# Prelude of a decoder layer: how the squares of the input are summed, what is loaded first, and how the first two projection tiles advance

## The chip, the cores and the metric

The kernel runs on one core of a Trainium2 chip, as one launch. The metric is the time on the device in microseconds (us), from start to end of the launch; smaller is better. Every input is float32, and the inputs lie in the chip's memory (HBM) when the launch starts.

## The reference

One hybrid decoder layer over 1024 tokens of width 1024. The conditioning vector `c` gives six modulation vectors. Then come an RMS norm with modulation, one input projection to 2240 columns, two kinds of attention (8 stick-breaking heads and 4 latent-attention heads), an output projection, a second norm with modulation, and a SwiGLU feed-forward of width 2816. Only its first lines touch this change:

```python
mod = jax.nn.silu(c) @ w_ada[l] + b_ada[l]
shift1, scale1, gate1, shift2, scale2, gate2 = [m[:, None, :] for m in jnp.split(mod, N_MOD, axis=-1)]
h = rms_norm(x, norm_attn[l]) * (1.0 + scale1) + shift1
proj = h @ w_in[l]
```

## The kernel before

The activations are kept transposed: `x_in[:, j, :]` is chunk j of eight, 128 channels on the partitions by 1024 tokens. A product of two float32 operands at close to full precision is made of three faster ones: an operand is split into a high part (a copy rounded to `fp32r`) and a low part (the difference), and the kernel sums high·high, high·low and low·high. `WH`/`WL` are the parts of a weight tile of 128 output channels, each with two buffers; `hH`/`hL` are those of the normalized input. A projection tile is 8 chunks x 3 products x 2 halves of 512 tokens = 48 matmuls, into two of the eight PSUM banks of `ps`.

Each engine runs its own list of instructions in the written order, and semaphores tie the lists together. What the prelude does before the first projection tile, in that order:

- SyncE (SP) starts the loads: three small ones, `x_in` in four parts of 1 MB, the raw weights of tiles 0 and 1 (`raw`, 0.5 MB each), then `ada1`, the four parts (2 MB each) of the modulation weights for `shift1` and `scale1`. Part g serves chunks 2g and 2g+1.
- ScalarE (ACT) squares each chunk as it comes (line 658). VectorE (DVE) adds the squares up in `sqs` (line 1112), seven additions. TensorE (PE) turns the sum by eight transposes (line 1721) and DVE reduces it (line 1122) to the mean square `ms` of each token (line 1124).
- GpSimd (POOL) takes the power -1/2 (line 557), DVE lays it on diagonals (line 1129), and PE spreads it over all partitions by two matmuls with ones (line 1749). DVE multiplies each chunk by it (`normalize`, line 1142).
- For part g, PE multiplies `silu(c)` with the modulation weights (`mod1_rows`, line 1734), DVE copies the result (`mod1_copy`, line 1119), PE sums the copy into columns by matmuls whose stationary side is a 128x128 block and whose moving side is one column of ones (`mod1_columns`, line 1741), and DVE makes shift and scale of it (`scale_shift`, lines 1136 and 1139). `mod1_rows(g)` waits for `scale_shift(g-2)`.
- Before `mod1_rows(0)` PE runs `WARM` = 40 small bf16 matmuls on the identity (line 1745), whose result nobody reads. A like group of 44 stands at line 1897, much later.
- For each chunk j, ACT writes `hH` (line 666) and then `x_in` scaled and shifted (line 667), and DVE writes `hL` as their difference (`h_low`, line 1147).

PE then advances tile 0 with chunk n as soon as `hH` of n is there (lines 1769 and 1780). Tile 1 follows three chunks behind (`LAG = 3`, by `half_chunk`, lines 1690 to 1692), so that it ends after tile 0. The parts 1 to 3 of the modulation lie between these chunks. Tiles 2 and up run as whole tiles (`proj_tile`, line 1701).

After the last `hL`, a line of its own starts: POOL clears `acc2` (line 563), whose place `x_in` had until then. SP then loads 2 MB of the second modulation weights (`ada2`), DVE adds them in (`ada_step`, line 1189), and only behind that does DVE split the weights of tile 3 (`wsplit`, line 1106). ACT makes `WH` of tile 2 (line 648) once tile 0 has ended, since the two share a buffer, and DVE its `WL`.

Of the kernel before, what the change touches and what calls it, by code (L numbers as in the profile page):

```python
# [15 lines left out]
F32 = mybir.dt.float32  # L16
# [3 lines left out]
ALU = mybir.AluOpType  # L20
ACT = mybir.ActivationFunctionType
AX = mybir.AxisListType

P = 128
S = 1024
D = 1024
NT = S // P
KD = D // P
# [6 lines left out]
EPS = 1e-6  # L35
# [72 lines left out]
LAG = 3  # L108
QKL = {6: (0, 1), 7: (1, 1), 8: (0, 2), 9: (1, 2), 10: (2, 1), 11: (3, 1), 12: (2, 2), 13: (4, 1)}
NM, NS = MH // 2 * NU, SBH // 2 * NU  # L110
WARM = 40
WARM_MLA = 44
BLOCKS = [NT - i for _, i in UNITS]
G0 = [(b + 1) // 2 for b in BLOCKS]
# [19 lines left out]
def build(nc, xT, cols_d, rows_d, pos_d, ada1_d, ada2_d, win_d, qup_d, kvup_d, wout_d, gu_d, down_d, x2_d, t_d, qkl_d, out_d):  # L134
# [3 lines left out]
    def at(name, shape, dt, kb):  # L138
        return nc.alloc_sbuf_tensor_at(name, shape, dt, offset=base + int(kb * 1024))


    ident = at("ident", [P, P], F32, 0)
# [41 lines left out]
    lowT = at("lowT", [P, 6, S], F32, 82)  # L184
    ada1 = at("ada1", [P, KD // 2, KD, 4 * P], F32, 34)
    acc1 = [at(f"acc1{s}", [P, 4 * P], F32, 102 + 2 * s) for s in range(2)]
    sqs = at("sqs", [P, S], F32, 194)
    x_in = at("x_in", [P, KD, S], F32, 106)
    sq = [at(f"sq{s}", [P, S], F32, 198 + 4 * s) for s in range(2)]
    diag1 = at("diag1", [P, NT, P], F32, 98)  # L190
# [99 lines left out]
    def pair(b, n=S):  # L290

        return ps[:, b:b + 2, :].rearrange("p b n -> p (b n)")[:, 0:n]

    names = """small_in pool_const trig_args trig_done silu_c_done x_sq x_add x_turned stat_ms stat_r stat_diag stat_bc silu_zero ada_part acc1_done mod1_mm a1_done
        xr_done h_done hH_done hL_done split_h split_l pe_tile in_evac ada2_in ada_acc mod2_mm mod2_sum low_sq low_add low_mm low_done
        dve hl_done lh_done ll_done q_mm kv_mm q_sq k_sq q_ms q_r k_ms q_copied rk_done kv_free kr_mm kr_sq kr_ms kr_r kr_rot kr_turn kr_out k_scaled work_done tr_done
        t_act t_dve v_mm v_even v_odd kr_zero left_one kr_h kr_l
# [87 lines left out]
    def _(sp):  # L385
        def load_raw(r, par, i, src):

            if not (isinstance(r, int) and r < 2):
                sp.wait_ge(sem["split_h"], r - 1)
                sp.wait_ge(sem["split_l"], r - 1)  # L390
            sp.dma_start(raw[par % 2][:, 0:src.shape[-1]], src).then_inc(raw_in[par % 2], 16)
# [3 lines left out]
        sp.dma_start(pos_i[:], pos_d).then_inc(sem["small_in"], 16)  # L395
        for k in range(4):
            sp.dma_start(x_in[:, 2 * k:2 * k + 2, :], xT[2 * k:2 * k + 2].rearrange("j p n -> p j n")).then_inc(xin_in[k], 16)
        for j in range(2):
            load_raw(j, j, 0, win_d[j])
        for g in range(KD // 2):  # L400
            sp.dma_start(ada1[:, g], ada1_d[g]).then_inc(ada1_in[g], 16)
        step = 0
        def load_ada(s):

# [233 lines left out]
    def _(act):  # L638
# [14 lines left out]
        A(silu_w[:, :, 0:1], cols[:, C_C:C_C + KD].unsqueeze(2), ACT.Silu).then_inc(sem["silu_c_done"], 1)  # L653
        for j in range(KD):
            act.wait_ge(xin_in[j // 2], 16)
            if j >= 3:
                act.wait_ge(sem["x_add"], j - 2)
            A(sq[j % 2][:] if j else sqs[:], x_in[:, j, :], ACT.Square).then_inc(sem["x_sq"], 1)
        split(0, 0, 0)
        split(1, 1, 0)  # L660
        act.wait_ge(sem["trig_args"], 1)
        A(trig[:], ang[:], ACT.Sin).then_inc(sem["trig_done"], 1)
        for j in range(KD):
            act.wait_ge(sem["xr_done"], j + 1)
            act.wait_ge(sem["a1_done"], j // 2 + 1)
# [396 lines left out]
    def _(dve):  # L1062
# [40 lines left out]
        def wsplit(h, par):  # L1103
            r = raw_index(par)
            dve.wait_ge(sem["split_h"], h + (r - par) + 1)
            V.tensor_tensor(WL[par % 2][:], raw[r % 2][:], WH[par % 2][:], ALU.subtract).then_inc(sem["split_l"], 1)  # L1106

        for j in range(1, KD):
            dve.wait_ge(sem["x_sq"], j + 1)
            if j >= 2:  # L1110
                dve.wait_ge(sem["x_add"], j - 1)
            V.tensor_tensor(sqs[:], sqs[:], sq[j % 2][:], ALU.add).then_inc(sem["x_add"], 1)

        def mod1_copy(g):

            dve.wait_ge(sem["ada_part"], g + 1)
            if g >= 2:
                dve.wait_ge(sem["mod1_mm"], g - 1)
            V.tensor_copy(acc1[g % 2][:], ps[:, 4 + g % 2, :]).then_inc(sem["acc1_done"], 1)

        dve.wait_ge(sem["x_turned"], 1)
        ch(V.reduce_sum(rss[:], pair(4).rearrange("p (t n) -> p t n", t=NT), axis=AX.X))
        ch.sync()
        V.tensor_scalar(ms[:, 0, :], rss[:], 1.0 / D, EPS, ALU.mult, ALU.add).then_inc(sem["stat_ms"], 1)
        wsplit(0, 0)
        dve.wait_ge(sem["stat_r"], 1)
        for hf in range(2):
            t = slice(4 * hf, 4 * hf + 4)
            V.tensor_tensor(diag1[:, t, :], ident[:].unsqueeze(1).broadcast_to([P, 4, P]), rms[:, 0, t].unsqueeze(2).broadcast_to([P, 4, P]), ALU.mult).then_inc(sem["stat_diag"], 1)
        wsplit(1, 1)  # L1130

        def scale_shift(g):

            dve.wait_ge(sem["mod1_mm"], g + 1)
            j = slice(2 * g, 2 * g + 2)
            ch(V.tensor_tensor(mod1[:].rearrange("p (s j) -> p s j", s=2)[:, :, j], ps[:, 4 + g % 2, 0:4].rearrange("p (s j) -> p s j", s=2),
                               cols[:, C_B:C_B + 16].rearrange("p (s j) -> p s j", s=2)[:, :, j], ALU.add))
            ch.sync()
            V.scalar_tensor_tensor(a1[:, j], mod1[:, 8 + 2 * g:10 + 2 * g], 1.0, cols[:, C_GA + 2 * g:C_GA + 2 * g + 2], ALU.add, ALU.mult).then_inc(sem["a1_done"], 1)

        def normalize(j):
            V.tensor_tensor(x_in[:, j, :], x_in[:, j, :], pair(6), ALU.mult).then_inc(sem["xr_done"], 1)
# [4 lines left out]
            V.tensor_tensor(hL[:, j, :], x_in[:, j, :], hH[:, j, :], ALU.subtract).then_inc(sem["hL_done"], 1)  # L1147

        mod1_copy(0)
        dve.wait_ge(sem["stat_bc"], 2)  # L1150
        normalize(0)
        scale_shift(0)
        normalize(1)
        for g in range(KD // 2):
            if 2 * g + 2 < KD:
# [527 lines left out]
    def _(pe):  # L1683
# [32 lines left out]
            ins.then_inc(sem["stat_bc"], 1)  # L1716

        pe.wait_ge(sem["pool_const"], 10)
        pe.wait_ge(sem["x_add"], KD - 1)
        for tt in range(NT):  # L1720
            last = nc.tensor.transpose(ps[:, 4 + tt // 4, tt % 4 * P:(tt % 4 + 1) * P], sqs[:, tt * P:(tt + 1) * P], ident[:])
        last.then_inc(sem["x_turned"], 1)

        def mod1_rows(g):

# [33 lines left out]
                proj_tile(t, t0 + u, 2 * u, hH, hL)  # L1759


        pe.wait_ge(sem["split_l"], 2)
        for n in range(KD + LAG):
            if n < KD:
                w = slice(n * P, (n + 1) * P)
                pe.wait_ge(sem["hH_done"], n + 1)
                for k, l in enumerate((WH, WL)):
                    for hf in range(2):
                        mm(ps[:, hf, :], l[0][:, w], hH[:, n, 512 * hf:512 * hf + 512], start=(n == 0 and k == 0), stop=False)
            if n % 2 == 0 and n // 2 + 1 < KD // 2:  # L1770
                mod1_rows(n // 2 + 1)
            if n >= LAG:
                for hf in range(2):
                    last = half_chunk(1, 2, hf, n - LAG, hH, hL)
            if n % 2 == 0 and n // 2 + 1 < KD // 2:
                mod1_columns(n // 2 + 1)
            if n < KD:
                pe.wait_ge(sem["hL_done"], n + 1)
                for hf in range(2):
                    last = mm(ps[:, hf, :], WH[0][:, w], hL[:, n, 512 * hf:512 * hf + 512], start=False, stop=(n == KD - 1))  # L1780
                if n == KD - 1:
                    last.then_inc(sem["pe_tile"], 1)
        last.then_inc(sem["pe_tile"], 1)
        repeat(pe, 2, lambda i: in_pair(2, i))
        in_pair(6, 0)
        def low_sums(k):
# [504 lines left out]
```

## Time and profile before

| | |
|---|---|
| Time, median of 3 runs | 1360.83 us (1360.55 to 1362.74) |
| Time of the profiled execution | 1363.38 us |
| Its span, first to last instruction | 1361.6 us |
| PE busy | 1301.8 us (96%), 6708 matmul pieces |
| DVE, ACT, POOL busy | 810.5, 554.9 and 63.4 us |
| Read from and written to HBM | 117.77 and 24.12 MB |

The profile is of one execution. All times in it count from the start of its span. A float32 matmul whose operands aren't rounded runs as two pieces, each with its own weight load (`PEld`); one of `fp32r` operands, or a transpose, as one. The time of a piece is longer than the distance to the next one, since pieces overlap: what a group costs is the distance from start to start.

### The profile page before, as it was taken

The page shows a single profiled execution, that of the slowest core. Times are in us where ns is not written, and L with a number is a line of the kernel's source. Part 1 is how long each engine was busy: PE and PEld are TensorE (multiplying, and loading weights), DVE is VectorE, ACT ScalarE, POOL GpSimd, SP SyncE. Part 2 cuts the span into 40 slices and gives each one's busy share as a digit, 9 for nine tenths or more (in the row PEclk, how much of TensorE's full clock was granted, in tenths as well). Part 3 has the DMA queues.
Part 4 walks back from the last instruction along what each step waited for, and adds up shares of the span by engine and source line. Part 5 has one row for each costly group of instructions (what it writes and reads, how often), then busy time and mean ns, then how long its engine had stood idle before and what let it go on. Part 6 is the DMA issues. An engine that isn't in the chain of part 4 may idle for free.

```text
span 1361.6 us, 17167 instructions
## 1 busy us (share of the span) xinstructions
PE 1301.8 (96%) x6708; PEld 1083.3 (80%) x6708; DVE 810.5 (60%) x1118; ACT 554.9 (41%) x890; POOL 63.4 (5%) x71
## 2 busy tenths in 40 slices
PE   3999999998999999899989999999999999999998
PEld 2678888896888888788867888888888888887886
DVE  7534567686556888953588665566655643334333
ACT  4512312585435778861275333333333322232221
POOL 1100200131000001000000000000000000001001
PEclk9999999999999999999999999999999999999999
DMA  9253445100011333401042212222122145447443
GB/s 382 72 231 124 168 188 188 49 1 1 2 39 40 78 79 77 171 16 62 32 185 93 93 63 78 93 93 89 56 89 93 62 145 183 154 145 262 140 145 126
DMA packets 38989, 149.25 MB, mean 110 GB/s; under 512 B 4352, under 2 KB 4480, under 8 KB 37376
## 3 DMA queue, kind: packets, MB, share of 16 engines
q1 hardware_dynamic: 36576, 139.80, 29.9%
q0 software_dynamic: 2336, 8.39, 1.7%
q8 instruction: 52, 0.85, 0.3%
q14 instruction: 25, 0.20, 0.0%
HBM read 117.77 MB, written 24.12 MB: 104 GB/s over the span
## 4 chain that ended last, share of the span: by engine, by line
PE 84%; DVE 8%; issue 3%; ACT 3%; DMA 1%; POOL 1%; SPq 0%; DVEq 0%; ACTq 0%
PE ps L2189 28%; PE ps L1701 13%; PE ps L1690 10%; PE ps L1692 10%; PE ps L1691 10%; DVE left L1408 3%; PE ps L1966 2%; PE ps L1944 2%; PE ps L1933 1%; PE ps L1953 1%; PE ps L1911 1%; DMA ada<-ada 1%; DVE beta L1413 1%; PE ps L1734 1%; ACT omb L907 1%
## 5 line engine op out<-in xcount | busy, mean ns | idle before, releaser
L1690 PE MATMUL ps<-TH,dWH 128*128 128x512 f32 x352 | 137.1, 390 | 0.9 <-DVE yst L1665 0.9
L1692 PE MATMUL ps<-TH,dWL 128*128 128x512 f32 x352 | 137.0, 389 | 0.0
L1691 PE MATMUL ps<-TL,dWH 128*128 128x512 f32 x352 | 136.9, 389 | 0.0
L2189 PE MATMUL ps<-h2H,slH 128*128 128x512 f32 x320 | 124.6, 389 | 0.0
L2189 PE MATMUL ps<-h2H,slL 128*128 128x512 f32 x320 | 124.5, 389 | 0.0
L2189 PE MATMUL ps<-h2L,slH 128*128 128x512 f32 x320 | 124.5, 389 | 0.0
L1624 DVE TENSOR_TENSOR TL<-traw,TH 128x512 fp32r<-128x512 f32 x44 | 30.5, 693 | 134.5 <-ACT TH L1029 134.5
L1009 ACT ACTIVATE slH<-ssum 128x512 fp32r<-128x512 f32 x80 | 50.4, 632 | 140.4 <-PE ps L2189 96.4
L1029 ACT ACTIVATE TH<-traw 128x512 fp32r<-128x512 f32 x44 | 27.8, 632 | 164.1 <-PE ps L1692 155.6
L1408 DVE TENSOR_TENSOR_SCAN left<-omb 128x255 f32<-128x255 f32 (+5 forms) x64 | 86.4, 1350 | 10.8 <-ACT omb L907 10.8
L1690 PEld LDWEIGHTS ps<-TH,dWH 128*128 128x128 f32 x352 | 66.1, 188 | 15.2 <-DVE yst L1665 1.3
L1692 PEld LDWEIGHTS ps<-TH,dWL 128*128 128x128 f32 x352 | 66.1, 188 | 13.8
L1691 PEld LDWEIGHTS ps<-TL,dWH 128*128 128x128 f32 x352 | 66.1, 188 | 13.7
L1966 PE MATMUL ps<-VS,wT 128*128 128x64 f32 x576 | 71.5, 269 | 0.3 <-DVE o_sb L1394 0.3
L2189 PEld LDWEIGHTS ps<-h2H,slH 128*128 128x128 f32 x320 | 60.1, 188 | 12.7 <-issue 0.3
L2189 PEld LDWEIGHTS ps<-h2L,slH 128*128 128x128 f32 x320 | 60.1, 188 | 12.5
L2189 PEld LDWEIGHTS ps<-h2H,slL 128*128 128x128 f32 x320 | 60.1, 188 | 12.4
L1966 PEld LDWEIGHTS ps<-VS,wT 128*128 128x128 f32 x576 | 69.4, 192 | 0.5 <-DVE o_sb L1394 0.5
L1602 DVE TENSOR_TENSOR slL<-ssum,slH 128x512 fp32r<-128x512 f32 x80 | 54.9, 688 | 18.2 <-ACT slH L1009 18.2
L1106 DVE TENSOR_TENSOR WL<-raw,WH 128x1024 fp32r<-128x1024 f32 x34 | 43.2, 1269 | 32.3 <-ACT WH L648 32.2
L1602 DVE TENSOR_TENSOR slL<-sraw,slH 128x512 fp32r<-128x512 f32 x60 | 41.2, 689 | 35.4 <-ACT slH L1009 35.4
L1626 DVE TENSOR_TENSOR dWL<-draw,dWH 128x1024 fp32r<-128x1024 f32 x44 | 53.9, 1225 | 11.0 <-ACT dWH L1031 11.0
(325 smaller groups left out, 3030.1 us busy)
## 6 DMA issues: line engine op xcount, KB each, us to landing
ada<-ada SPq DMA_DIRECT2D x12, 2048.0 KB, 9.1
draw<-down SPq DMA_DIRECT2D x44, 512.0 KB, 3.7
sraw<-gu SPq DMA_DIRECT2D x20, 1024.0 KB, 5.9
raw<-win SPq DMA_DIRECT2D x22, 512.0 KB, 4.5
traw<-t_spill_d SPq DMA_DIRECT2D x44, 256.0 KB, 3.9
t_spill_d<-tst SPq DMA_DIRECT2D x20, 512.0 KB, 3.0
x_in<-xT SPq DMA_DIRECT2D x4, 1024.0 KB, 8.6
qkl_spill_d<-qkl SPq DMA_DIRECT2D x8, 512.0 KB, 3.4
```

The lines of the kernel that those rows point to most:

```text
L1009: A(slH[q][:], operand(u, q), ACT.Copy).then_inc(sem["g_h"], 1)
L1106: V.tensor_tensor(WL[par % 2][:], raw[r % 2][:], WH[par % 2][:], ALU.subtract).then_inc(sem["split_l"], 1)
L1408: V.tensor_tensor_scan(left[v % 2][:, 1:n], omb[v % 2][:, 0:n - 1], omb[v % 2][:, 0:n - 1], 1.0, ALU.mult, ALU.bypass).then_inc(sem["s_sca ...
L1602: V.tensor_tensor(slL[q][:], operand(u, q), slH[q][:], ALU.subtract).then_inc(sem["g_l"], 1)
L1624: V.tensor_tensor(TL[d % 2][:], traw[d % 2][:], TH[d % 2][:], ALU.subtract).then_inc(sem["tl_done"], 1)
L1626: V.tensor_tensor(dWL[d % 2][:], draw[d % 2][:], dWH[d % 2][:], ALU.subtract).then_inc(sem["d_l"], 1)
L1690: mm(out, lh, rh, start=first, stop=False)
L1691: mm(out, lh, rl, start=False, stop=False)
L1692: return mm(out, ll, rh, start=False, stop=last)
L1701: last = mm(ps[:, b + hf, :], l[s][:, j * P:(j + 1) * P], cut(r, j, half(hf)), start=(j == 0 and k == 0), stop=(j == KD - 1 and k == 2))
L1966: last = mm(ps[:, bank, c:c + SBD], wT[v % 2][:, k * P:(k + 1) * P], VS[:, qt + k, (2 * i + e) * SBD:(2 * i + e + 1) * SBD], start=(k == 0 ...
L2189: last = mm(ps[:, Q_BANK[q], :], l[q][:, w], r[:, c, :], start=(c == 0 and k == 0 and q not in (Q_G2, Q_S4)), stop=(c == 3 and k == 2), sk ...
```

## The change

Five edits, all ahead of tile 2:

1. The squares of a chunk are no longer added by DVE. PE takes each 128x128 block of the square as the stationary side against one column of ones, 8 products for each chunk, 64 in all, and accumulates in 8 columns of PSUM bank 5. Semaphore `x_mm` counts chunks. The transposes, the reduction and the buffer `sqs` are gone. ACT, with two buffers for the squares, waits for `x_mm` from the third chunk on.
2. `WARM` is 12 instead of 40.
3. Part 0 of `ada1` is loaded ahead of the two raw weight tiles.
4. The order on ACT and DVE changes: ACT computes the sine table ahead of the two weight splits; DVE makes the two `WL` after `mod1_copy(0)` and after `scale_shift(0)`, instead of ahead of and behind the diagonals.
5. PE advances tiles 0 and 1 together, chunk by chunk: `high(n)` is the 8 products with `hH` of chunk n, `low(n)` the 4 with `hL`, and `mod1_rows` and `mod1_columns` are put between other ones of them. Both tiles end with `low(7)`.

```diff
-WARM = 40
+WARM = 12
...
-        for j in range(2):
-            load_raw(j, j, 0, win_d[j])
         for g in range(KD // 2):
             sp.dma_start(ada1[:, g], ada1_d[g]).then_inc(ada1_in[g], 16)
+            if g == 0:
+                for j in range(2):
+                    load_raw(j, j, 0, win_d[j])
...
-            if j >= 3:
-                act.wait_ge(sem["x_add"], j - 2)
-            A(sq[j % 2][:] if j else sqs[:], x_in[:, j, :], ACT.Square).then_inc(sem["x_sq"], 1)
+            if j >= 2:
+                act.wait_ge(sem["x_mm"], j - 1)
+            A(sq[j % 2][:], x_in[:, j, :], ACT.Square).then_inc(sem["x_sq"], 1)
+        act.wait_ge(sem["trig_args"], 1)
+        A(trig[:], ang[:], ACT.Sin).then_inc(sem["trig_done"], 1)
         split(0, 0, 0)
         split(1, 1, 0)
-        act.wait_ge(sem["trig_args"], 1)
-        A(trig[:], ang[:], ACT.Sin).then_inc(sem["trig_done"], 1)
...
-        for j in range(1, KD):
-            dve.wait_ge(sem["x_sq"], j + 1)
-            if j >= 2:
-                dve.wait_ge(sem["x_add"], j - 1)
-            V.tensor_tensor(sqs[:], sqs[:], sq[j % 2][:], ALU.add).then_inc(sem["x_add"], 1)
...
-        dve.wait_ge(sem["x_turned"], 1)
-        ch(V.reduce_sum(rss[:], pair(4).rearrange("p (t n) -> p t n", t=NT), axis=AX.X))
-        ch.sync()
-        V.tensor_scalar(ms[:, 0, :], rss[:], 1.0 / D, EPS, ALU.mult, ALU.add).then_inc(sem["stat_ms"], 1)
-        wsplit(0, 0)
+        dve.wait_ge(sem["x_mm"], KD)
+        V.tensor_scalar(ms[:, 0, :], ps[:, 5, 0:NT], 1.0 / D, EPS, ALU.mult, ALU.add).then_inc(sem["stat_ms"], 1)
...
-        wsplit(1, 1)
...
         mod1_copy(0)
+        wsplit(0, 0)
         dve.wait_ge(sem["stat_bc"], 2)
         normalize(0)
         scale_shift(0)
+        wsplit(1, 1)
         normalize(1)
...
-        pe.wait_ge(sem["x_add"], KD - 1)
-        for tt in range(NT):
-            last = nc.tensor.transpose(ps[:, 4 + tt // 4, tt % 4 * P:(tt % 4 + 1) * P], sqs[:, tt * P:(tt + 1) * P], ident[:])
-        last.then_inc(sem["x_turned"], 1)
+        for j in range(KD):
+            pe.wait_ge(sem["x_sq"], j + 1)
+            for tt in range(NT):
+                last = mm(ps[:, 5, tt:tt + 1], sq[j % 2][:, tt * P:(tt + 1) * P], ones[:, 0:1], start=(j == 0 and tt == 0), stop=(j == KD - 1), skip_group_check=True)
+            last.then_inc(sem["x_mm"], 1)
...
+        def high(n):
+
+            w = slice(n * P, (n + 1) * P)
+            pe.wait_ge(sem["hH_done"], n + 1)
+            for u in range(2):
+                if n == 0:
+                    pe.wait_ge(sem["split_l"], u + 1)
                 for k, l in enumerate((WH, WL)):
                     for hf in range(2):
+                        mm(ps[:, 2 * u + hf, :], l[u][:, w], hH[:, n, 512 * hf:512 * hf + 512], start=(n == 0 and k == 0), stop=False)
+
+        def low(n):
+
+            w = slice(n * P, (n + 1) * P)
+            pe.wait_ge(sem["hL_done"], n + 1)
+            for u in range(2):
                 for hf in range(2):
+                    last = mm(ps[:, 2 * u + hf, :], WH[u][:, w], hL[:, n, 512 * hf:512 * hf + 512], start=False, stop=(n == KD - 1))
                 if n == KD - 1:
                     last.then_inc(sem["pe_tile"], 1)
+
+        high(0)
+        mod1_rows(1)
+        high(1)
+        mod1_columns(1)
+        low(0)
+        mod1_rows(2)
+        low(1)
+        mod1_columns(2)
+        high(2)
+        mod1_rows(3)
+        high(3)
+        mod1_columns(3)
+        low(2)
+        low(3)
+        high(4)
+        for n in range(5, KD):
+            high(n)
+            low(n - 1)
+        low(KD - 1)
```

## Rows read from the trace of the kernel before

**Rows 1.** The page, part 4: the chain that ended last, by engine.
```profile
PE 84%; DVE 8%; issue 3%; ACT 3%; DMA 1%; POOL 1%; SPq 0%; DVEq 0%; ACTq 0%
```

**Rows 2.** The chain in order of time, 0 to 75 us: start, length, what.
```profile
10.18 1.06 ACT sq L658
...
17.91 1.24 DVE sqs L1112
...
19.28 1.94 PE ps L1721 x8
21.22 4.07 PE ps L1745 x40
25.29 1.85 PE ps L1734 x16
27.15 1.93 PE ps L1749 x4
```

**Rows 3.** The timeline, 0 to 32 us: start, length, instruction, idle time before it.
```profile
7.63 1.06 ACT L658 ACTIVATE sqs<-x_in 128x1024 f32<-128x1024 f32 x1 [3.67 <-DMA x_in<-xT]
...
15.30 1.06 ACT L658 ACTIVATE sq<-x_in 128x1024 f32<-128x1024 f32 x1 [0.33 <-DMA x_in<-xT]
...
22.84 2.51 POOL L557 TENSOR_TENSOR rms<-ms,nhalf 128x8 f32<-128x8 f32 x1 [19.58 <-DVE ms L1124]
...
25.39 1.29 DVE L1129 TENSOR_TENSOR diag<-ident,rms 128x512 f32<-128x512 f32 x2 [1.57 <-POOL rms L557]
...
27.74 0.68 DVE L1119 COPY acc<-ps 128x512 f32<-128x512 f32 x1
...
30.68 1.24 ACT L666 ACTIVATE hH<-x_in,mod,a 128x1024 fp32r<-128x1024 f32 x1 [10.64 <-DVE a L1139]
```

**Rows 4.** The same chain, behind the last hL.
```profile
61.62 3.54 POOL acc L563
65.18 8.27 DMA ada<-ada
```

**Rows 5.** The timeline from 63 to 80 us: between tiles 0 and 3.
```profile
63.45 1.06 ACT L648 ACTIVATE WH<-raw 128x1024 fp32r<-128x1024 f32 x1 [3.22 <-PE ps L1780]
...
64.54 1.23 DVE L1106 TENSOR_TENSOR WL<-raw,WH 128x1024 fp32r<-128x1024 f32 x1 [2.99 <-ACT WH L648]
...
67.27 0.62 PE L1701 MATMUL ps<-hH,WH 128*128 128x512 f32 x2
...
73.47 4.49 DVE L1189 SCALAR_TENSOR_TENSOR acc<-ada,silu_c,acc 128x4096 f32<-128x4096 f32 x1 [7.71 <-DMA ada<-ada]
...
79.24 0.70 PE L1701 MATMUL ps<-hH,WH 128*128 128x512 f32 x2 [0.93 <-DVE WL L1106]
```

**Rows 6.** PE's groups by shape, whole span: busy us, mean ns of one piece.
```profile
L1745 PE MATMUL ps<-identb 128*128 128x128 bf16 x40 | 4.3, 306 | 0.0
...
L1741 PE MATMUL ps<-ones,acc 128*128 128x1 f32 x32 | 4.0, 246 | 1.6 <-DVE acc L1119 1.6
...
L1897 PE MATMUL ps<-identb 128*128 128x128 bf16 x44 | 2.6, 219 | 0.0
...
L1721 PE MATMUL ps<-ident,sqs 128*128 128x128 f32 x8 | 1.9, 424 | 19.3 <-DVE sqs L1112 19.3
```

**Rows 7.** Stretches: length, busy us (instructions) of each engine, PEclk, DMA share, GB/s.
```profile
0.00:31.00 31.00, 10.56 (x76) 7.95 (x76) 21.23 (x31) 12.56 (x15) 4.82 (x16) 1.00 0.94 377
32.00:33.00 1.00, 0.93 (x2) 0.83 (x3) 0.85 (x1) 1.00 (x2) 0.00 (x0) 0.50 1.07 459
35.00:36.00 1.00, 1.00 (x16) 0.22 (x8) 0.00 (x0) 0.32 (x1) 0.00 (x0) 0.90 1.14 475
36.00:300.00 264.00, 260.60 (x1256) 215.86 (x1249) 155.97 (x198) 98.36 (x137) 30.86 (x21) 1.00 0.35 129
```

**Rows 8.** Weight loads of line 1769, 31 to 35 us, then 36 to 50 us.
```profile
L1769 PEld LDWEIGHTS ps<-hH,WH x2: 288/313/338, 32.0 to 32.2; 128*128 128x128 f32 x2
...
L1769 PEld LDWEIGHTS ps<-hH,WH x8: 186/188/189, 38.6 to 49.3; 128*128 128x128 f32 x8
```

More of the change, by code:

```diff
@@ L186, in build @@
     acc1 = [at(f"acc1{s}", [P, 4 * P], F32, 102 + 2 * s) for s in range(2)]
-    sqs = at("sqs", [P, S], F32, 194)
     x_in = at("x_in", [P, KD, S], F32, 106)
@@ L292, in pair @@
         return ps[:, b:b + 2, :].rearrange("p b n -> p (b n)")[:, 0:n]
-    names = """small_in pool_const trig_args trig_done silu_c_done x_sq x_add x_turned stat_ms stat_r stat_diag stat_bc silu_zero ada_part acc1_done mod1_mm a1_done
+    names = """small_in pool_const trig_args trig_done silu_c_done x_sq x_mm stat_ms stat_r stat_diag stat_bc silu_zero ada_part acc1_done mod1_mm a1_done
         xr_done h_done hH_done hL_done split_h split_l pe_tile in_evac ada2_in ada_acc mod2_mm mod2_sum low_sq low_add low_mm low_done
@@ L1759, in in_pair @@
                 proj_tile(t, t0 + u, 2 * u, hH, hL)
[L1762 to L1766, printed above, removed]
+        def high(n):
[4 more added lines that the diff above has]
+                    pe.wait_ge(sem["split_l"], u + 1)
                 for k, l in enumerate((WH, WL)):
                     for hf in range(2):
[L1769 to L1772, printed above, removed]
-                for hf in range(2):
[L1774 to L1780, printed above, removed]
+                        mm(ps[:, 2 * u + hf, :], l[u][:, w], hH[:, n, 512 * hf:512 * hf + 512], start=(n == 0 and k == 0), stop=False)
[3 more added lines that the diff above has]
+            for u in range(2):
+                for hf in range(2):
+                    last = mm(ps[:, 2 * u + hf, :], WH[u][:, w], hL[:, n, 512 * hf:512 * hf + 512], start=False, stop=(n == KD - 1))
                 if n == KD - 1:
                     last.then_inc(sem["pe_tile"], 1)
-        last.then_inc(sem["pe_tile"], 1)
+        high(0)
[17 more added lines that the diff above has]
+        low(KD - 1)
         repeat(pe, 2, lambda i: in_pair(2, i))
```

## Prediction

> **What bounds the kernel now.** I read the page first. PE is busy for nearly the whole span, and the chain that ended last is PE's for the most part [rows 1]: behind the prelude, the kernel is a queue of matmuls. So whatever moves the moment at which PE gets going moves the end by as much, and nothing else in this change can. Next, the chain in order of time over the first 75 us. Squares come from ACT at the pace of the input, seven additions on DVE follow them and end at 19.15, then PE's transposes, 40 warm-up matmuls, `mod1_rows(0)` and the broadcast [rows 2]. The reader is to see that PE does nothing of use before 19.28. Then the timeline of the same stretch: `ms` is there when POOL starts, 22.84, and the first `hH` ends at 30.68 + 1.24 = 31.92, so 9.1 us lie between [rows 3]. Last, what stands at the other end: tile 3 starts at 79.24 after an idle 0.93 us, because its `WL` waits behind `ada_step(0)` [rows 5], and that hangs on the last `hL` by 3.54 us of clearing and 8.27 us of loading [rows 4]. From there PE runs on without a gap that the prelude could fill. My yardstick is therefore the start of tile 3: the change is worth 79.24 minus its new value. Two lines lead there: tile 0's end, then `WH` and `WL` of tile 2, then 48 matmuls; and the last `hL`, then memset, load, `ada_step` and `WL` of tile 3.
>
> **PE's clock, since much hangs on it.** The same bf16 matmul ran at (4.3 - 0.3) / 39 = 0.10 us each in the warm-up at 21 us and at (2.6 - 0.2) / 43 = 0.055 us at line 1897 [rows 6]: PE was at half pace in its first 6 us of work (19.28 to 25.29 [rows 2]), though the granted clock reads 1.00 there [rows 7]; no event had been recorded yet. It was recorded at half (1.2 of 2.4 GHz) once more, from about 31.7 to 35.1, behind an idle stretch before the first `hH` [rows 7]. That second rise came some 3.1 us after PE had resumed at 32.0. These two, 3.1 and 6 us, are my bounds for how long the new first work of PE runs at half pace, if it raises the clock as those matmuls did.
>
> **Part by part.**
>
> *Sum of squares.* Removed: the seventh addition's tail, transposes and reduction, so `ms` no longer waits until 22.7. Added: 64 products in 128 pieces. The nearest row is line 1741, the same shape in the same form: four groups of 8 pieces, (4.0 - 4 x 0.25) / 28 = 0.107 us from piece to piece at full pace [rows 6]. At half pace no such row exists; the transposes, one-piece 128x128 loads too, ran at (1.9 - 0.42) / 7 = 0.21 us [rows 6], which is just double, so I take 0.214. The bounds of the whole are 128 x 0.107 = 13.7 us and 128 x 0.214 = 27.4 us. The first square is there at 8.7 [rows 3], PE starts at 8.8. A square takes ACT 1.06 us and the input brings one each 1.3 us (two parts between 10.18 and 15.30 [rows 2, 3]), while eight products take 1.7 us at best: PE is the slower one and never starves, and ACT's new wait for `x_mm` costs nothing as the buffer it wants is free one chunk ahead. Queued behind ACT's last square are sine and splits, needed only 6 us later. With 3.1 us at half pace, 14.5 pieces are done by 11.9 and the other 113.5 take 12.1: the end, T, is 24.0. With 6 us, 28 pieces are done by 14.8 and 100 take 10.7: T = 25.5. I take the middle, T = 24.8. `ms` follows at T + 0.3 = 25.1, against 22.8 before. So this step loses 2.3 us: the sum was following the input closely (last addition at 19.15), and PE can't.
>
> The row for what a weight load does at half clock is that of line 1769: 313 ns in the slow stretch, 188 ns after it [rows 8]. The Trainium skill says otherwise (TensorE: Matmul & The Clock Gate, section "LDWEIGHTS (loading the stationary operand)"): a load takes its columns over 1.2, whatever the clock. By that rule 0.107 us would hold at either clock, T would be 22.5 and the step would cost nothing; this trace disagrees, and I go by it, but keep the rule's outcome as a rival.
>
> *WARM, load order, split order.* From `ms`: POOL 2.51 (with 0.15 to start), two diagonals 1.29, copy 0.68 [rows 3], `WL` of tile 0 1.23 [rows 5], `normalize(0)` and `scale_shift(0)` 1.22 and 0.36 of the same kind and place as before, `hH` 1.24: T + 9.0. PE's part is hidden behind it: 12 warm-ups 0.7 us (1.3 at half pace), `mod1_rows(0)` 1.85, both by T + 3.5, when the first diagonal is ready; the second broadcast ends at T + 5.4, `WL` at T + 6.1. Before, 40 warm-ups and `mod1_rows(0)` kept the broadcast until 27.15. From `ms` to the first `hH` it is now 8.7 us in place of 9.1: 0.4 gained. Part 0 of `ada1` lands at 15.3 + 2.56 x 2 = 20.4, the raw tiles at 23, wanted only at T and later: the load order is worth nothing, and if `ada1` part 0 had stayed behind them (23) it would have been in time as well. The other parts land as before.
>
> *Tiles 0 and 1 together.* A product costs (79.24 - 0.93 - 67.27) / 48 = 0.23 us [rows 5], so `high` is 1.85, `low` 0.92, `mod1_rows` 1.9, `mod1_columns` 1.0. PE at full pace, from T + 9.1: high(0) 10.95, rows(1) 12.9, high(1) 14.7, columns(1) 15.7, low(0) 16.6, rows(2) 18.5, low(1) 19.4. Here it waits: columns(1) lets DVE end `scale_shift(1)` at 16.4; ACT's two passes for chunk 2 end at 18.8, `h_low(2)` at 20.05, and only then DVE copies for columns(2), 20.75. PE: columns(2) 21.8, high(2) 23.6, rows(3) 25.5, high(3) 27.4; the same loop again holds columns(3) until 28.0, so 29.0, low(2), low(3) 30.8, high(4), high(5), low(4) 35.4, then high(6), low(5), high(7), low(6) and low(7) to T + 41.8, with tile 0 ending at 41.3. The last `hL` ends at T + 36.6 (ACT's and DVE's two passes for chunks 6 and 7 after `scale_shift(3)` at T + 30.7). Tile 1 no longer ends late behind tile 0, and that has a price: before, tile 1's last 16 matmuls covered the `WH` and `WL` of tile 2 (63.45 to 65.77, PE went on at 67.27 without idling [rows 5]). Now PE idles for them, T + 41.3 to T + 43.9, about 2 us net. Tile 2 then ends at T + 43.9 + 11.0 = T + 54.9. The other line gives T + 36.6 + 3.6 + 8.3 + 4.5 + 1.3 = T + 54.3 [rows 4, 5], slightly earlier: hidden, but with 0.6 us to spare. With T = 24.8 tile 3 starts at 79.7.
>
> *The slow stretch.* Before, PE idled 2.2 us ahead of the first `hH` and the clock fell; high(0) and rows(1) then took some 1.6 us longer, which is in the 79.24. Now PE idles from T + 6.4 to T + 9.1, 2.7 us, with 0.6 us more idle ahead of the broadcast, so I expect the same fall. It costs high(0) up to 8 x 0.2 = 1.6 us and rows(1) a little, and both stand on the path: between 0 and 2.2 us, I take 1.5.
>
> Sum: 79.7 + 1.5 = 81.2, or +2.0 us, against 1363.38 for the profiled execution. The median shown lies 2.5 us under that, and I carry the difference over: 1360.8 + 2.0 = 1362.8.
>
> The Trainium skill has a rule that speaks against leaning on these products at all (the same page, "What's actually happening"): the throttled clock is the default, and PE's activity releases it. No row shows the clock rising under products of one moving column; that is the first rival.
>
> **Rivals.** A change under 0.2% (2.7 us) is what a measurement of this kernel can't tell from none.
>
> 1. *The products never raise the clock.* They keep PE at half pace: T = 8.8 + 27.4 + 0.2 = 36.4, 11.6 us later than I take, and broadcast and columns are slow too (some 3 us). Tile 3 starts at 79.7 + 14 = 93 to 95: +14 to +16, about 1375.5. For it: both rises in the trace came under other matmuls, none under this form. Against it: the one-column groups of line 1741 are short and lie amid other work, so they say nothing either way, and PE is without a pause from 8.8 us on. It decides from the point where the half pace lasts past 9 us.
> 2. *The half pace lasts somewhat longer than 6 us,* or the second slow stretch falls on high(0) fully: each us of it adds 0.5. From +2.0 it takes 1.4 us more of half pace to pass 2.7: +2.7 to +5, about 1364.5.
> 3. *Faster.* The loads keep their pace at half clock (T = 22.5), the clock doesn't fall again (-1.5) and DVE's copies aren't late: 22.5 + 54.9 = 77.4, less up to 1.5 us for the waits ahead of columns(2) and (3): -1.8 to -3.3, about 1358.2. Speaking for it: less work on DVE. Against: rows 8, and the idle time.
> 4. *Nothing moves:* the sums above cancel (+-0.5); it is part of the likeliest case.
>
> **How the numbers follow.** My forecast (from -2 to +2.7) 0.50; rival 2 0.15; rival 1 0.23; rival 3 with more than 2.7 us gained 0.12. Its own range is 1359.5 to 1364.0. The range for all takes in rival 1's price, and leaves out most of rival 3 and of what lies beyond rival 1: 1359.2 to 1376.0. Faster 0.12, same 0.50, slower 0.38.
>
> **What would show it.** The products' pace from 8.8 us on: 0.21 us at first, then 0.107, and where it turns. T near 24.8, first `hH` at T + 9. PE idle for 2 us ahead of tile 2, waiting for `WL`. Tile 3 starting with no wait on `ada_step`. The forecast is wrong if the turn never comes, or if the products run at full pace from the start.

## The result, and the profile after

The changed kernel took 1379.39 us (median of 4 runs, 1378.24 to 1380.70) against 1361.78 for the kernel before: ratio 1.0118, 95% interval 1.0104 to 1.0133. It is 1.2% slower (the two medians by themselves give 1.013). My forecast was no change, 1362.8; the result lies above my whole range and some 4 us above the price I had put on the first rival, which is what happened. Some 1 us of that is no error of the sum: the kernel before, which I carried over at 1360.83, had a median of 1361.78 in these runs.

The page of the changed kernel, part 4, answers to [rows 1]: PE's share of the chain has grown.

```profile
PE 87%; DVE 7%; issue 3%; ACT 2%; DMA 0%; POOL 0%; SPq 0%; DVEq 0%; ACTq 0%
```

The chain in order of time, start, length and what, answers to [rows 2 and 4]:

```profile
8.61 27.44 PE ps L1714 x128
36.05 1.30 PE ps L1738 x12
37.35 2.63 PE ps L1727 x16
39.98 1.93 PE ps L1742 x4
...
43.52 1.25 ACT hH L666
...
44.81 3.06 PE ps L1764 x8
47.88 2.54 PE ps L1727 x16
...
59.17 3.34 PE ps L1764 x8
...
80.92 1.24 DVE WL L1106
...
82.29 17.76 PE ps L1693 x70
```

The reader is to see one line: 128 pieces of one-column products (line 1714) take 27.44 us, 0.214 us each from the first to the last. Before, the whole way from the first square to the end of the transposes ended at 21.2; here PE finishes at 36.05.

The same group by itself: length of a piece (least, median, most), and who waited.

```profile
L1714 PEld LDWEIGHTS ps<-ones,sq x128: 289/333/338, 8.6 to 35.6; 128*128 128x128 f32 x128
L1714 PE MATMUL ps<-ones,sq x128: 345/352/353, 8.6 to 35.7; 128*128 128x1 f32 x128
...
  DVE ms L1116: 26.7, 1
  ACT sq L658: 14.6, 6
```

A weight load takes 333 ns, near the 313 ns of the slow stretch in [rows 8], and even the least, 289 ns, is far above the 188 ns behind it: no piece ran at full pace. ACT, which before was paced by the input, waited 14.6 us for PE to free its two buffers. That cost nothing on the path, since PE never stood idle for a square.

The timeline, answering to [rows 3 and 5]: start, length, instruction, idle time before it.

```profile
36.41 1.67 POOL L557 TENSOR_TENSOR rms<-ms,nhalf 128x8 f32<-128x8 f32 x1 [33.15 <-DVE ms L1116]
...
43.52 1.24 ACT L666 ACTIVATE hH<-x_in,mod,a 128x1024 fp32r<-128x1024 f32 x1 [10.73 <-DVE a L1129]
...
79.83 1.06 ACT L648 ACTIVATE WH<-raw 128x1024 fp32r<-128x1024 f32 x1 [7.28 <-PE ps L1772]
...
80.92 1.22 DVE L1106 TENSOR_TENSOR WL<-raw,WH 128x1024 fp32r<-128x1024 f32 x1 [7.04 <-ACT WH L648]
82.29 0.70 PE L1693 MATMUL ps<-hH,WH 128*128 128x512 f32 x2 [2.11 <-DVE WL L1106]
```

The new wait ahead of tile 2 is there as forecast, 2.11 us. And the granted clock (the column behind POOL) was at half three times behind the products, where the kernel before had it once in the same stretch of work:

```profile
46.00:49.00 3.00, 3.00 (x13) 1.37 (x15) 1.96 (x2) 2.16 (x2) 0.00 (x0) 0.50 0.40 150
59.00:63.00 4.00, 4.00 (x14) 2.48 (x17) 2.69 (x5) 2.31 (x3) 0.00 (x0) 0.57 0.00 0
83.00:87.00 4.00, 4.00 (x12) 3.09 (x12) 1.24 (x1) 0.66 (x1) 0.00 (x0) 0.57 0.69 250
```

The account, from profile to profile (spans 1378.5 and 1361.6, 16.9 us apart). As the end of tile 2 I take the start of its copy out of PSUM on ACT; the timeline of the kernel before, then of the one after:

```profile
78.45 1.02 ACT L673 ACTIVATE lowT<-ps 128x1024 f32 x1 [9.01 <-PE ps L1701]
```

```profile
95.21 1.03 ACT L673 ACTIVATE lowT<-ps 128x1024 f32 x1 [11.55 <-PE ps L1693]
```

| stretch | before | after | difference |
|---|---|---|---|
| start to POOL's power (`ms` ready) | 22.84 | 36.41 | +13.6 |
| from there to the end of the first `hH` | 9.1 | 8.35 | -0.7 |
| from there to the end of tile 2 | 46.5 | 50.45 | +3.9 |
| wait ahead of tile 3 | 0.9 | none | -0.9 |
| everything behind | | | +1.0 |

So 13.6 of 16.9 us are the sum of squares. The last line goes with a longer slow stretch ahead of attention, behind a place where PE idles 3.0 us in both kernels: from 312 to 320 us the kernel before was granted 0.89 and then 0.69, and this one, at the same place in its work,

```profile
328.00:332.00 4.00, 2.62 (x10) 2.46 (x11) 3.93 (x11) 2.44 (x5) 0.00 (x0) 0.63 0.00 0
332.00:336.00 4.00, 4.00 (x14) 3.19 (x14) 0.23 (x2) 0.46 (x2) 0.00 (x0) 0.52 0.01 2
```

That this is all of the 1.0 us was not tested. Its length is no mark of the change either: the run with only the sum changed (below) has the same loss and only the short one.

### The profile page after: what moved, and what is told of

It reads as the page before. It is cut to its first block, busy times and chain, and to the rows that moved or that the text cites. A ratio compares the mean times of both kernels' runs of the same rounds, so it can differ in the third digit from the quotient of the medians.

```text
span 1378.5 us, 17338 instructions
## 1 busy us (share of the span) xinstructions
PE 1329.9 (96%) x6800; PEld 1109.5 (80%) x6800; DVE 800.8 (58%) x1110; ACT 555.0 (40%) x890; POOL 62.7 (5%) x71
## 4 chain that ended last, share of the span: by engine, by line
PE 87%; DVE 7%; issue 3%; ACT 2%; DMA 0%; POOL 0%; SPq 0%; DVEq 0%; ACTq 0%
PE ps L2200 28%; PE ps L1693 14%; PE ps L1682 10%; PE ps L1684 10%; PE ps L1683 10%; DVE left L1400 3%; PE ps L1977 2%; PE ps L1955 2%; PE ps L1714 2%; PE ps L1944 1%; PE ps L1964 1%; PE ps L1764 1%; PE ps L1922 1%; DVE beta L1405 1%; ACT omb L907 1%
## 5 line engine op out<-in xcount | busy, mean ns | idle before, releaser
L1684 PEld LDWEIGHTS ps<-TH,dWL 128*128 128x128 f32 x352 | 66.1, 188 | 13.8
L2200 PEld LDWEIGHTS ps<-h2L,slH 128*128 128x128 f32 x320 | 60.1, 188 | 12.4
L1693 PE MATMUL ps<-hH,WH 128*128 128x512 f32 x192 | 59.9, 393 | 2.1 <-DVE WL L1106 2.1
```

What stands on the lines that cost most here:

```text
L1684: return mm(out, ll, rh, start=False, stop=last)
L1693: last = mm(ps[:, b + hf, :], l[s][:, j * P:(j + 1) * P], cut(r, j, half(hf)), start=(j == 0 and k == 0), stop=(j == KD - 1 and k == 2))
L2200: last = mm(ps[:, Q_BANK[q], :], l[q][:, w], r[:, c, :], start=(c == 0 and k == 0 and q not in (Q_G2, Q_S4)), stop=(c == 3 and k == 2), sk ...
```

## The experiments

Theory A: one-column products neither raise PE's clock nor hold it, so the sum runs at half pace throughout, and that is the bulk; the joint advance of tiles 0 and 1 costs a little more by its idle time. Rival B: the new order of tiles and the 12 warm-ups cost the bulk. Rival C: the clock can't rise so early after the launch, whatever PE does. Each kernel was timed against the kernel before on the same chip.

### The sum back on DVE

The changed kernel, with the additions, transposes and reduction of before.

```diff
-        for j in range(KD):
-            pe.wait_ge(sem["x_sq"], j + 1)
-            for tt in range(NT):
-                last = mm(ps[:, 5, tt:tt + 1], sq[j % 2][:, tt * P:(tt + 1) * P], ones[:, 0:1], ...)
+        pe.wait_ge(sem["x_add"], KD - 1)
+        for tt in range(NT):
+            last = nc.tensor.transpose(ps[:, 4 + tt // 4, ...], sqs[:, tt * P:(tt + 1) * P], ident[:])
```

> Everything of the change stays, but the squares are added on DVE and turned by eight transposes, as before the change. Theory A (the one-column products never raise PE's clock, and that is the bulk of the loss): ms at 22.5 to 22.8 us in place of 36.3, and 1363 to 1366 us, what is left over the kernel before being the joint advance of tiles 0 and 1 (2 us of idle ahead of tile 2, more slow stretches). Rival B (the new order of tiles 0 and 1 and the 12 warm-ups cost the bulk): 1372 us or more.

Measured: 1365.31 us (1359.88 to 1367.36, 10 runs), ratio 1.0015 (1.0001 to 1.0029). Nearly all of the loss is gone, as A has it, and B falls. The profiled execution was the fastest of the ten, and its chain shows why: no slow stretch falls between the tiles.

```profile
30.21 2.14 PE ps L1772 x8
...
63.49 1.24 DVE WL L1107
...
64.86 45.16 PE ps L1702 x198
```

High(0) takes 2.14 us in place of 3.06, and tile 2 starts at 64.86. Its span is 1358.1 us; the 3.5 us under the profile before compare a fastest execution with a middle one, and the median is above the kernel before. PE's wait ahead of tile 2 is there all the same:

```profile
64.86 0.70 PE L1702 MATMUL ps<-hH,WH 128*128 128x512 f32 x2 [2.10 <-DVE WL L1107]
```

It waits 2.30 us ahead of high(0) and 0.89 us ahead of columns(2) as well, as long as in the changed kernel (2.13 and 0.87), and no slow stretch follows any of the three. So such waits alone don't bring one on every time. The spread of 7.5 us over the ten runs leads to the last experiments, from the joint advance alone onward.

### Only the sum changed

The kernel before with the one-column products and nothing else of the change: 40 warm-ups, loads, splits and tiles as they were.

> The kernel before with only the sum of squares changed to one-column products (40 warm-ups, order of loads, of splits and of tiles 0 and 1 as before). Theory A: the products run at 0.214 us throughout, ms at 36.3 us, 13.6 later than before; 40 warm-ups at half pace now end at 40.3 and hold up mod1_rows(0); 1375 to 1377 us. Rival B: below 1368 us.

Measured: 1379.91 us (1378.51 to 1380.81), ratio 1.0128 (1.0106 to 1.0149), about 3 us above the 1375 to 1377 expected. Its chain:

```profile
8.76 27.44 PE ps L1713 x128
36.20 4.29 PE ps L1737 x40
40.49 2.25 PE ps L1726 x16
```

The same 27.44 us, and this one edit carries the whole 1.2%: the intervals of this run and of the changed kernel overlap, so the other edits together are worth too little to tell. Tile 3 starts at 94.58 here and at 94.90 in the changed kernel. The way there differs, though: here the path goes through `ada_step(0)`, and PE waits 0.54 us for the `WL` of tile 3.

### Warm-ups ahead of the products

The changed kernel, with 48 small bf16 matmuls while PE has nothing to do.

```diff
+        for _ in range(48):
+            mm(ps[:, 0, 0:P], identb[:], identb[:], start=True, stop=True)
         for j in range(KD):
             pe.wait_ge(sem["x_sq"], j + 1)
```

> The changed kernel with 48 small bf16 matmuls on the identity ahead of the one-column products, in time in which PE has nothing to do (3.4 to 8.6 us at half pace). If the products neither raise nor hold the clock: they start at full pace, 0.107 us from piece to piece, for some us, then fall to 0.214; the last ends between 28 and 35 us, time 1371 to 1378 us. If they hold a clock that is up once (rival): they end at 22.5 to 23.5 us, time 1363 to 1366 us. If the clock can't rise this early whatever PE does (rival C): 36 us, 1379 us.

Measured: 1378.85 us (1373.84 to 1379.02), ratio 1.0109 (1.0081 to 1.0136). The last product ended at 33.05, inside what A has. The time did not follow: the median lies 0.9 us above A's 1371 to 1378 and can't be told from the changed kernel's, though one of the four executions took 1373.84. In the traces the lead over the changed kernel is 3.0 us at the last product, 2.7 at 1130 us and 1.4 at the end; PE waits 1.1 us in the last stage for `dWL`, which it doesn't in the changed kernel. As to the clock, this run shows the mechanism best. The products' pieces first between 8.6 and 12.2 us, then between 12.8 and 30 us:

```profile
L1716 PEld LDWEIGHTS ps<-ones,sq x32: 192/192/292, 8.7 to 12.2; 128*128 128x128 f32 x32
...
L1716 PEld LDWEIGHTS ps<-ones,sq x81: 333/333/333, 12.8 to 29.9; 128*128 128x128 f32 x81
```

and the granted clock, which here was recorded (next to last columns as before):

```profile
11.00:12.00 1.00, 1.00 (x11) 1.00 (x11) 0.00 (x0) 0.85 (x1) 0.00 (x0) 1.00 1.03 422
12.00:13.00 1.00, 1.00 (x8) 1.00 (x7) 0.00 (x0) 0.33 (x1) 0.00 (x0) 0.62 1.03 418
13.00:14.00 1.00, 1.00 (x7) 1.00 (x6) 0.00 (x0) 0.73 (x1) 0.00 (x0) 0.50 1.04 418
```

PE was busy for 1.00 of each of these microseconds, and yet the clock fell from 2.4 to 1.2 GHz between 12 and 13 us and was at half until the products were over. The clock can be up at 8.7 us, so C falls; and a PE that the profile calls busy all the time isn't one whose clock stays up. The same rows answer the rule I had weighed (the Trainium skill, TensorE: Matmul & The Clock Gate, section "LDWEIGHTS (loading the stationary operand)", columns over 1.2). The page names no clock there; that the figure holds at either clock was my reading. The loads took 192 ns at full pace and 333 at half, so the trace disagrees with that reading.

### Wide products

The same sums with the operands exchanged: ones stand, the squares move, 512 columns in each piece. DVE takes the means off the diagonal blocks.

```diff
-            for tt in range(NT):
-                last = mm(ps[:, 5, tt:tt + 1], sq[j % 2][:, tt * P:(tt + 1) * P], ones[:, 0:1], ...)
+            for hf in range(2):
+                last = mm(ps[:, 6 + hf, :], ones[:], sq[j % 2][:, 512 * hf:512 * hf + 512], start=(j == 0), stop=(j == KD - 1))
```

> The same sums, with ones as the stationary side and the squares as the moving side: 512 moving columns in each of 32 pieces in place of 1 in each of 128, 13.8 us in all at full pace and 27.4 at half, so the same work in time at either clock. DVE then picks the means out by one multiplication and one reduction, some 2.6 us more. Theory A: the clock rises 3 to 6 us after 8.6, the last product ends at 24 to 26 us, ms is there at 27 to 29, time 1368 to 1371 us. Rival C (the clock rises only late after the launch, whatever PE does): last product at 36, ms at 39, 1382 us.

Measured: 1370.10 us (1367.84 to 1371.15), ratio 1.0050 (1.0033 to 1.0068). The pieces from 9 to 12 us, then from 12.4 to 24 us:

```profile
L1719 PE MATMUL ps<-sq,ones x4: 734/1061/1190, 9.2 to 11.9; 128*128 128x512 f32 x4
...
L1719 PE MATMUL ps<-sq,ones x27: 592/592/593, 12.4 to 23.6; 128*128 128x512 f32 x27
```

By 12.4 us the pieces are down from 1061 to 592 ns: full pace 3.2 us after the first product, and the last ends at 24.6, in the 24 to 26 that A gave. At either clock this form costs as much PE time as the narrow one (13.8 or 27.4 us), it starts 0.6 us later and also from standstill. With the operands exchanged, 9 us are gained back. Two things change by that at once: a piece has 512 moving columns instead of one, and there are 32 weight loads instead of 128. The runs show that the one form raises the clock and the other doesn't, not which of the two differences does it.

### A few moving matmuls among the products

48 ahead as above, and 6 more after each chunk.

```diff
+            for _ in range(6):
+                mm(ps[:, 0, 0:P], identb[:], identb[:], start=True, stop=True)
```

> The changed kernel with 48 small bf16 matmuls ahead of the one-column products and 6 between each two chunks of them (0.33 us at full pace). If it takes only a few moving matmuls among the products to hold the clock: the products keep 0.107 us, the last ends at 25 to 26 us, 1366 to 1369 us. If the share of the products in the time decides, and 0.33 in 2 us is too little: the clock falls at 10 to 15 us as in the run with the warm-ups ahead alone, and the last ends at 34 to 38 us, 1377 to 1382 us. I hold the second for likelier.

Measured: 1382.54 us (1381.33 to 1385.11), ratio 1.0148 (1.0127 to 1.0169). On PE's timeline the third chunk is slow already:

```profile
11.01 2.22 PE L1716 MATMUL ps<-ones,sq 128*128 128x1 f32 x16
13.09 0.80 PE L1719 MATMUL ps<-identb 128*128 128x128 bf16 x6
13.68 3.52 PE L1716 MATMUL ps<-ones,sq 128*128 128x1 f32 x16
```

The six did not hold the clock; they only added their own time. The last product ended at 37.07, inside the 34 to 38 I had, and the median lies 0.5 us above my 1377 to 1382. Whether more of them would hold it wasn't tried.

### Only the joint advance

The kernel before with `high`/`low` in place of its loop over chunks, nothing else.

> The kernel before with only the order of tiles 0 and 1 on PE changed (both chunk by chunk). Theory A: the joint advance is worth about nothing by itself: it ends 1 to 2 us sooner where the clock stays up, and loses them to 2 us of idle ahead of tile 2 and to slow stretches behind such idle; ratio to before 0.998 to 1.003. Rival B (it is a real part of the loss): 1.004 or more. A real gain hidden by the sum of squares (rival D): below 0.998.

Measured: 1366.43 us (1361.07 to 1368.34, 12 runs), ratio 1.0017 (1.0005 to 1.0028), inside what A gave. The profiled execution shows where a gain goes: 2.1 us of idle ahead of tile 2, and two slow stretches instead of one.

```profile
44.00:48.00 4.00, 4.00 (x17) 2.77 (x20) 2.97 (x5) 2.03 (x2) 0.00 (x0) 0.57 0.00 0
68.00:72.00 4.00, 4.00 (x13) 3.10 (x11) 1.29 (x1) 0.95 (x2) 0.00 (x0) 0.57 0.72 272
```

In those four microseconds at 68 PE is busy for all four and gets 13 pieces done; in the four from 66 of the run with the sum on DVE, at full clock, it did 20. That run had the same 2.1 us of idle time in front, so here too the idle time is a suspect, not a shown cause.

### PE's idle time filled

If idle time lets the clock fall, small matmuls in it should bring the time back. First with the old order of tiles: 56 from about 13 us on, 12 behind the transposes, 36 ahead of the first `hH`.

```diff
-WARM = 40
+WARM = 12
...
+        pe.wait_ge(sem["x_add"], 2)
+        for _ in range(56):
+            mm(ps[:, 0, 0:P], identb[:], identb[:], start=True, stop=True)
         pe.wait_ge(sem["x_add"], KD - 1)
...
+        for _ in range(36):
+            mm(ps[:, 0, 0:P], identb[:], identb[:], start=True, stop=True)
         pe.wait_ge(sem["split_l"], 2)
```

> The kernel before with PE's idle time filled: 56 small bf16 matmuls from 12.5 us on, ahead of the transposes, 12 in place of 40 behind them, and 36 more in the wait ahead of the first hH. If moving matmuls raise and hold the clock: full pace from about 18.5 us, transposes 1 us shorter, mod1_rows(0) out of the broadcast's way, no slow stretch at 32 us (1.6 us in the trace of before): 3 to 4 us less, ratio 0.9965 to 0.998. If the fill only shifts the slow stretches elsewhere: within 0.1% of before.

Measured: 1361.13 us (1359.72 to 1364.29, 12 runs), ratio 0.9986 (0.9975 to 0.9997): faster than before, but by half of what I expected. Then the same with all of the change but its sum, and 36 more ahead of tile 2.

> Squares added on DVE, everything else of the change, and PE's idle time filled: 56 small matmuls from 12.5 us on ahead of the transposes, 36 ahead of the first hH, 36 in the 2 us ahead of tile 2. If idle time ahead of the joint tiles is what let the clock fall in most executions of the kernel with the sum on DVE: 1357 to 1360 us in nearly all runs, ratio 0.996 to 0.998, against 1.0015 without the fill. If not: a spread of 7 us and a ratio about 1.00 again.

Measured: 1359.96 us (1358.68 to 1362.45, 12 runs), ratio 0.9975 (0.9966 to 0.9985). This version beats both kernels, and the kernel with the sum on DVE (1.0015) by 0.4%. On PE's timeline, in the slowest of the twelve executions:

```profile
20.22 1.09 PE L1725 MATMUL ps<-ident,sqs 128*128 128x128 f32 x8 [1.44 <-DVE sqs L1113]
...
28.02 2.17 PE L1788 MATMUL ps<-identb 128*128 128x128 bf16 x36
30.45 0.73 PE L1775 MATMUL ps<-hH,WH 128*128 128x512 f32 x2 [0.27 <-ACT hH L667]
...
62.82 2.19 PE L1809 MATMUL ps<-identb 128*128 128x128 bf16 x36
65.08 0.70 PE L1702 MATMUL ps<-hH,WH 128*128 128x512 f32 x2
```

The eight transposes take 1.09 us, not 1.94 as in [rows 2], and both waits are closed but for 0.3 us. The prelude has no slow stretch in this trace; one from 311 to 318 us is still there.

### Four last questions

With the fill ahead of tile 2 taken out again:

> The filled kernel with the joint advance, without the 36 small matmuls in the 2 us ahead of tile 2. If that idle time is what lets the clock fall behind it: in a part of the executions a slow stretch at the start of tile 2, 1.7 us each time, so a median 0.5 to 1.7 us higher and a wider spread, ratio 0.9979 to 0.9988. If the idle time is too short to matter: 0.9975 and the same spread.

Measured: 1362.09 us (1359.20 to 1363.80, 12 runs), ratio 0.9988 (0.9978 to 0.9998). The median is 2.1 us higher than with the fill (by the ratios 1.8 us) and the spread is 4.6 us against 3.8. The fill can't start tile 2 any sooner, so what it pays, if this is more than noise, must come by the clock. But the intervals overlap a little, and the trace of this run doesn't show it: behind its 2.10 us of idle time the granted clock stays at 1.00 from 64 to 72 us, and its one slow stretch in the prelude lies at 43 to 47 us, where the run with the old loads below has one too, in spite of the fill. That the gap ahead of tile 2 costs clock in the slower executions is argued, not shown.

Part 0 of the modulation weights loaded first, with the old order of tiles (and filled):

> The run with the old order of tiles 0 and 1 and PE's idle time filled, and in addition part 0 of the modulation weights loaded ahead of the raw tiles (edit 3). There mod1_rows(0) waited 1.9 us for that part, so here it should start at 21.6 to 22 us instead of 23.3. If the load order is worth something once PE is ready sooner: 0.3 to 0.8 us less, ratio 0.9978 to 0.9984. If diagonals and copy hide it, as my prediction had it: 0.9986 again.

Measured: 1360.24 us (1359.27 to 1361.69), ratio 0.9981 (0.9972 to 0.9991), against 0.9986 without: in the direction of a gain, within the intervals. `mod1_rows(0)` did start sooner, at 22.12; in the run without, the load held it:

```profile
23.30 1.92 PE L1737 MATMUL ps<-ada,silu_w 128*32 128x512 f32 x16 [1.90 <-DMA ada<-ada]
```

And the raw tiles loaded first, with the joint advance:

> The filled kernel with the joint advance (ratio 0.9975), with the raw tiles loaded ahead of part 0 of the modulation weights again. mod1_rows(0) then waits for its load until 23.3 us instead of 22.8. If that is hidden: 0.9975 within 0.0008. If it shows: up to 0.5 us, 0.9979.

Measured: 1360.49 us (1358.92 to 1361.07), ratio 0.9978 (0.9970 to 0.9987) against 0.9975. In both pairs the new load order has the lower median, by 0.9 and 0.5 us; both differences stay below what these runs can tell.

Last, 98 in place of 44 small matmuls ahead of the first attention scores, where the other kernels idle 3.0 us near 310 us:

> The filled kernel with the joint advance, with 98 in place of 44 small matmuls ahead of the first latent-attention scores near 310 us, where PE sits idle 3.0 us in every kernel and the clock then falls for 3.4 or 6.8 us. If the fill holds the clock there: no slow stretch near 315 us, 1.5 to 3 us less than without, ratio 0.9950 to 0.9965. If it doesn't, or PE's queue delays the scores: 0.9975 or more.

Measured: 1359.61 us (1358.33 to 1361.87), ratio 0.9976 (0.9966 to 0.9986): no gain, a miss. The idle time and the slow stretch at that place are gone:

```profile
304.50 5.63 PE L1923 MATMUL ps<-identb 128*128 128x128 bf16 x98
...
312.00:316.00 4.00, 3.04 (x21) 2.49 (x20) 2.69 (x6) 1.61 (x5) 1.07 (x2) 1.00 0.00 0
316.00:320.00 4.00, 4.00 (x28) 3.38 (x28) 1.69 (x5) 2.14 (x8) 0.77 (x1) 1.00 0.00 0
...
336.00:340.00 4.00, 4.00 (x26) 4.00 (x25) 1.23 (x4) 0.84 (x3) 0.00 (x0) 0.64 0.00 0
```

The traces answer where the gain went, at least in part. My expectation took it that the clock falls behind this idle time in every kernel. It doesn't: the runs with the sum on DVE, with the gap open and both with another load order idle the same 3.0 us unfilled, are granted 1.00 from 312 to 320 us all the same, and fall to between 0.57 and 0.69 at 336 to 340 us, as this one does. So the fill removed a slow stretch that often isn't there, and the one at 336 us stayed.

## Why the prediction was wrong, by its own steps

**What bounds it, and the yardstick: right.** Nearly 16 of the 16.9 us had arrived at the start of tile 3.

**The sum of squares: this step failed.** Its bounds held; the upper one, 27.4 us, is the measured value to a tenth. What failed is the sentence "I take the middle": I let the half pace end after 3.1 to 6 us because the two rises in the trace had come so, though both had come under other matmuls. It lasted for all 27.4 us, and T came at 36.05 in place of 24.8, 11.3 us late. The one-column products never raise the clock (27.44 us in two kernels), don't hold one that is up (the run with warm-ups ahead), and the same sums with the operands exchanged raise it within 3.2 us. I had this as the first rival, at 0.23. By the rows alone the chance ought to have been higher: no row showed this form raising the clock, and the one recorded fall, at 31.7 us, came behind the group of line 1741 and an idle stretch. Which of the two brought it on can't be told. The range's upper end was the rival's mean price, not its bound, and so too low; its bound, 1376.8, would have been too low as well.

**The rival's price: 14 to 16 us forecast, nearly 16 measured at tile 3,** but by other terms. T was 36.05 (36.4 said), `ms` to first `hH` 8.35 us, so my 3 us for slow broadcast and columns were wrong: the clock was up again by then, behind the 12 warm-ups and most of `mod1_rows(0)` (1.93 us for the broadcast, as before). In their place came three slow stretches.

**From `ms` to the first `hH`: right in sign, by another way.** 0.7 us gained against 0.4. PE was not hidden as I had it: `mod1_rows(0)` took 2.63 us, and DVE's copy waited 0.65 us for it. What pays is POOL's power, which I left at 2.51 us and which took 1.67. That goes with the new order on DVE (edit 4), though no run changes it alone: before, the `WL` of tile 0 starts 0.24 us ahead of the power. DVE's line before, then two lines of the run with the old order of tiles and the new loads:

```profile
22.60 1.22 DVE L1106 TENSOR_TENSOR WL<-raw,WH 128x1024 fp32r<-128x1024 f32 x1
```

```profile
22.22 1.67 POOL L558 TENSOR_TENSOR rms<-ms,nhalf 128x8 f32<-128x8 f32 x1 [18.96 <-DVE ms L1125]
...
22.86 1.22 DVE L1107 TENSOR_TENSOR WL<-raw,WH 128x1024 fp32r<-128x1024 f32 x1 [0.80 <-ACT WH L649]
```

The power takes 2.51 or 2.52 us in the four traces in which this split starts just ahead of it, and 1.67 or 1.68 in the ten others. In one of these ten, the one shown, the split starts 0.64 us behind the power and costs it nothing.

**The joint advance: the wait ahead of tile 2 right** (2.11 us, 2 said), the other line through `ada_step` hidden, right. **The slow stretch: mis-sized.** I gave one stretch 1.5 us. There were three: high(0) and rows(1) 5.6 us instead of 3.75, high(2) 3.34 instead of 1.85, tile 2 12.8 instead of 11.0, together 5.1 us. Each lies behind a wait of PE (2.13, 0.87 and 2.11 us), and in the last two cases behind one that the joint advance made or moved; with only the sum changed there is one slow stretch in the prelude, as before. That the waits let the clock fall is argued, since the run with the sum on DVE has all three waits and no slow stretch behind them. Alone, this edit costs 0.17% (0.05 to 0.28).

**The load order is worth nothing: not refuted.** In the changed kernel the part was in time. My remark that it would have been in time either way holds there too, where the products end at 36 us; in the filled kernel with the old order of loads PE waited 1.90 us for it.

## What to carry to other kernels

"Busy" in a profile isn't what keeps TensorE fast: before small-column products are put on it, look whether its clock was up in the stretch they go to, and price them at half pace if they run alone. If a reduction over partitions must go on TensorE, let the data move and the ones stand; here that was still slower than adding on DVE (1370.10 us against 1365.31). Where a piece of work has a price at both clocks and no row shows which one it will get, both prices belong inside the range. Idle time of PE just ahead of dense work may be worth filling with matmuls that nobody reads, if they end before the data come: in the prelude the fills together paid 0.14% with the old order of tiles and 0.4% with the joint advance, near 310 us a fill paid nothing. So each has to be measured, over more than one execution.

## What the runs showed of the hardware that I had not expected

- A stream of weight loads, each with one moving column, busy without a pause, left TensorE at half clock for 27.44 us; with the clock up beforehand it fell within 4 us of such work (full at 8.7, granted 0.62 between 12 and 13 us).
- The same sums with 512 moving columns a piece and a quarter of the weight loads were at full clock 3.2 us after their start from standstill (pieces of 1061 ns, then 592).
- Six bf16 matmuls of 128 columns between two groups of 16 pieces didn't hold the clock.
- A fp32 weight load of 128 x 128 takes 192 ns at full and 333 ns at half clock.
- The granted clock of a profile can read 1.00 where it was at half: from 8 to 36 us the changed kernel shows 1.00 with every piece at half pace, and the first lower reading comes at 45 us. Piece lengths tell it.
- Behind 2.1 us of idle time ahead of tile 2, the granted clock averaged 0.57 over four microseconds in the changed kernel and with the joint advance alone, and stayed at 1.00 with the sum on DVE and with the gap left open (one trace each).
- POOL's power on 128 x 8 elements took 2.51 us with a DVE subtraction begun 0.24 us ahead of it, and 1.67 us with DVE idle or beginning 0.64 us behind.
